# Two-model kernel, one core: top-k rounds spread into the latent attention, the recurrence's mean among its units, a decay parameter and GpSimd's power table at other places, normalisation factors taken one product sooner

## What is computed

```python
score = einsum('bths,bth->bts', relu(iqb @ ik * idx_scale), wb)      # indexer of A, causal
_, sel = lax.top_k(score, topk)                                      # topk = 128
o = o_inter + o_intra ; o = rmsnorm(o, g_out)                        # recurrence B, mean over 64 channels
a_bar = exp(A * dt) ; b_bar = (a_bar - 1) / A * B                    # S5 of the even layer, and powers of a_bar
log_a = -RG_C * gate_r * softplus(-lam) ; a = exp(log_a)             # RG-LRU of the odd layer
```

## Time and profile before

| | us |
|---|---|
| median of 3 runs | 3545.89 (3545.56 to 3547.06) |
| the profiled execution | 3545.3 |
| its span in the profile | 3543.5 |
| PE busy | 3386.2 (96% of the span) |
| DVE, ACT, POOL busy | 1597.8 (45%), 1170.5 (33%), 409.4 (12%) |
| granted TensorE clock, mean | 0.977 of full |

### The profile page before, as it was taken

The page is one execution under the profiler, slowest core; times in us unless marked ns, Lnnn a source line. Parts: engine busy times, 40 slices in busy tenths (PEclk is TensorE's granted clock), DMA queues, the critical chain, the costliest instruction groups (busy, mean ns, idle before and its releaser), DMA issues.

```text
span 3543.5 us, 39704 instructions
## 1 busy us (share of the span) xinstructions
PE 3386.2 (96%) x14384; PEld 2598.6 (73%) x14384; DVE 1597.8 (45%) x2295; ACT 1170.5 (33%) x1727; POOL 409.4 (12%) x285
## 2 busy tenths in 40 slices
PE   7999998999999999999899999899899997899998
PEld 5888775778887888775677887565678885668886
DVE  3332498533323333388734332834333327543322
ACT  4232344433323332244433322213333223543322
POOL 1110002111100110001111100401111002111100
PEclk9999999999999999999999999899999998999999
DMA  4332231033333333232023332430233332123332
GB/s 135 95 95 95 83 79 43 1 89 95 93 92 94 89 95 95 89 84 61 1 66 89 95 95 88 93 74 30 60 89 95 95 94 78 54 75 93 93 95 77
DMA packets 420124, 286.04 MB, mean 81 GB/s; under 512 B 57416, under 2 KB 395180, under 8 KB 419884
## 3 DMA queue, kind: packets, MB, share of 16 engines
q1 hardware_dynamic: 419200, 283.62, 27.8%
q10 hardware_dynamic: 828, 1.13, 0.1%
HBM read 280.24 MB, written 4.47 MB: 80 GB/s over the span
## 4 chain that ended last, share of the span: by engine, by line
PE 89%; DVE 7%; ACT 2%; issue 2%; DMA 0%; POOL 0%; DVEq 0%; ACTq 0%; SPq 0%; POOLq 0%
PE bank L856 25%; PE bank L857 25%; PE bank L858 25%; PE bank L1266 1%; PE bank L1147 1%; PE bank L1165 1%; PE bank L1146 1%; PE bank L851 1%; PE bank L1260 1%; PE bank L1383 1%; DVE small L2078 1%; DVE arena L2080 1%; PE bank L996 0%; PE bank L998 0%; PE bank L997 0%
## 5 line engine op out<-in xcount | busy, mean ns | idle before, releaser
L858 PE MATMUL bank<-xn_lo,w_hi 128*128 128x512 f32 x2800 | 1098.5, 392 | 0.0
L856 PE MATMUL bank<-xn_hi,w_hi 128*128 128x512 f32 x2496 | 1001.5, 401 | 53.6 <-DVE xn_lo L1970 20.3
L1981 DVE TENSOR_TENSOR w_lo<-wring,w_hi 128x1024 fp32r<-128x1024 f32 x478 | 594.6, 1245 | 930.1 <-ACT w_hi L1509 929.2
L857 PE MATMUL bank<-xn_hi,w_lo 128*128 128x512 f32 x2496 | 990.4, 397 | 0.0
L1509 ACT ACTIVATE w_hi<-wring 128x1024 fp32r<-128x1024 f32 x490 | 517.6, 1059 | 1206.2 <-DMA wring<-in_ffn_down 357.9
L858 PEld LDWEIGHTS bank<-xn_lo,w_hi 128*128 128x128 f32 x2800 | 529.5, 189 | 132.8
L856 PEld LDWEIGHTS bank<-xn_hi,w_hi 128*128 128x128 f32 x2496 | 470.5, 188 | 176.8 <-issue 61.3
L857 PEld LDWEIGHTS bank<-xn_hi,w_lo 128*128 128x128 f32 x2496 | 471.4, 189 | 104.7 <-issue 2.6
L857 PE MATMUL bank<-h_hi,w_lo 128*128 (+1 forms) x1056 | 421.3, 399 | 0.0
L856 PE MATMUL bank<-h_hi,w_hi 128*128 (+1 forms) x1056 | 416.1, 394 | 0.0
L858 PE MATMUL bank<-h_lo,w_hi 128*128 (+1 forms) x1056 | 414.0, 392 | 0.0
(11 more groups left out here) (383 smaller groups left out, 2956.2 us busy)
## 6 DMA issues: line engine op xcount, KB each, us to landing
wring<-in_ffn_gate SPq DMA_DIRECT2D x88, 512.0 KB, 3.8
wring<-in_ffn_up SPq DMA_DIRECT2D x88, 512.0 KB, 3.8
wring<-in_ffn_down SPq DMA_DIRECT2D x88, 512.0 KB, 3.5
wring<-in_ffn_w_gate SPq DMA_DIRECT2D x44, 512.0 KB, 3.8
wring<-in_ffn_w_up SPq DMA_DIRECT2D x44, 512.0 KB, 3.8
wring<-in_ffn_w_down SPq DMA_DIRECT2D x44, 512.0 KB, 3.5
wring<-in_w_in SPq DMA_DIRECT2D x34, 512.0 KB, 3.7
wring<-in_w_out SPq DMA_DIRECT2D x16, 512.0 KB, 3.5
```

The source lines that it names most:

```text
L856: nc.tensor.matmul(ps, w_hi[:, slot, t, 0:M], hi, start=start, stop=False)
L857: nc.tensor.matmul(ps, w_lo[:, slot, t, 0:M], hi, start=False, stop=False)
L858: return nc.tensor.matmul(ps, w_hi[:, slot, t, 0:M], lo, start=False, stop=stop)
L1981: nc.vector.tensor_tensor(w_lo[:, slot, :, :].rearrange("p k c -> p (k c)"), wunit[:, slot, :], w_hi[:, slot, :, :].rearrange("p k c -> p ...
```

## The change

Six edits.

1. `Z_RSTD`: ACT takes factors 0 and 1 at unit dcq1, 2 and 3 at dckv, 4 and 5 at bq; none at bk.
2. `act_norm`: the table load for Sigmoid stands before the last chunk's copy, not before the first.
3. Top-k: passes 0 to 8 of the mixers' loop have 2, 2, 1, 1, 1, 1, 1, 1, 1 rounds, then 4 follow, and the last 12 stand one each in the attention's units i = 2 to 13.
4. Recurrence B: its output is made in banks 4 and 5, after one wait for all of DVE's blocks; both means are made in bank 5 at units 3 and 5, the factors on ACT at i = 4 and 6, the norm on DVE at i = 5 and 7. `Y_HYB` puts the convolution's chunks first.
5. The chain on `spc` moves to the even layer: its first two operations ahead of the parameters, the Exp beside them, and the other 17 behind the states, before the rotation of queries and keys.
6. GpSimd's power table waits for DVE's last `x_pow`, not for `par` = 40.

The diff, without the lines that only renumber waits and with the moved chain shortened:

```diff
-Z_RSTD = {"dcq1": (0,), "dckv": (1,), "bq": (2, 3), "bk": (4, 5)}
+Z_RSTD = {"dcq1": (0, 1), "dckv": (2, 3), "bq": (4, 5)}
...
-Y_HYB, Y_EVEN, Y_ODD = [2, 3, 4, 5, 6, 7, 0, 1], [4, 5, 6, 7, 0, 1, 2, 3], list(range(KD))
+Y_HYB, Y_EVEN, Y_ODD = [4, 5, 2, 3, 6, 7, 0, 1], [4, 5, 6, 7, 0, 1, 2, 3], list(range(KD))
...
             pe.e.wait_ge(dh_sq.h, dh_sq.by(pe.l, 16))
+            pe.e.wait_ge(at_sb.h, at_sb.by(pe.l, 2 * TB))
             for pr in range(2):
                 for tb in range(TB):
-                    pe.e.wait_ge(at_sb.h, at_sb.by(pe.l, 2 * (tb + 1)))
...
-                        nc.tensor.matmul(pb[pr][64 * q:64 * q + 64, tb * P:(tb + 1) * P], b_values[:, tb, h * B_VAL:(h + 1) * B_VAL],
+                        nc.tensor.matmul(pb[4 + pr][64 * q:64 * q + 64, tb * P:(tb + 1) * P], b_values[:, tb, h * B_VAL:(h + 1) * B_VAL],
...
-            pe_out_mean(pe, 0)
...
         def pe_out_mean(pe, pr):
 
-            pe.e.wait_ge(o_sq.h, o_sq.by(pe.l, pr + 1))
-            pe.e.wait_ge(u_msk.h, u_msk.by(pe.l, NCH - 1))
-            nc.tensor.matmul(pb[6 + pr][:, :], C("blk64"), T(t_osq[pr]), start=True, stop=True).then_inc(on_ps.h, 1)
+            pe.e.wait_ge(o_sq.h, o_sq.by(pe.l, 2))
+            if pr:
+                pe.e.wait_ge(on_ln.h, on_ln.by(pe.l, 1))
+            nc.tensor.matmul(pb[5][:, :], C("blk64"), T(t_osq[pr]), start=True, stop=True).then_inc(on_ps.h, 1)
...
         def hyb_ready(eng, u):
-            if u == 1:
-                pe_out_mean(eng, 1)
+            if u in (3, 5):
+                pe_out_mean(eng, (u - 3) // 2)
             if u == 2:
+                eng.e.wait_ge(o_sq.h, o_sq.by(eng.l, 1))
...
-            if u == 3:
+            if u == 8:
                 eng.e.wait_ge(on_ln.h, on_ln.by(eng.l, 2))
...
             if st:
-                nc.scalar.preload_act_table(ACT.Sigmoid)
                 for k in range(KD):
+                    if k == KD - 1:
+                        nc.scalar.preload_act_table(ACT.Sigmoid)
...
         def hyb_out_factor(act, i):
-            if i in (1, 2):
-                act.e.wait_ge(on_ps.h, on_ps.by(act.l, i))
-                rstd(act, pb[6 + i - 1][:, :], T(t_or[i - 1]), on_ln, on_r, i)
+            if i in (4, 6):
+                pr = (i - 4) // 2
+                act.e.wait_ge(on_ps.h, on_ps.by(act.l, pr + 1))
+                rstd(act, pb[5][:, :], T(t_or[pr]), on_ln, on_r, pr + 1)
...
             act.e.wait_ge(pro_sb.h, 2 + 4)
             nc.scalar.activation(c_dt, c_ldt, ACT.Exp).then_inc(par_act.h, 1)
+            act.e.wait_ge(sp_step.h, 2)
+            nc.scalar.activation(spc[:, 1, :], spc[:, 0, :], ACT.Exp, scale=-1.0).then_inc(par_act.h, 1)
...
         def act_odd(act):
-            act.e.wait_ge(sp_step.h, 2)
-            nc.scalar.activation(spc[:, 1, :], spc[:, 0, :], ACT.Exp, scale=-1.0).then_inc(par_act.h, 1)
...
         HEAD_TOP = sum(Z_ROUNDS)
-        HEAD_PART = 2
+        HEAD_ROUNDS = [2, 2, 1, 1, 1, 1, 1, 1, 1]
+        HEAD_END = HEAD_TOP + sum(HEAD_ROUNDS)
+        END_ROUNDS = 4
...
-                top = HEAD_TOP + i * HEAD_PART
-                dve_top(dve, top, top + HEAD_PART)
-            dve_top(dve, top + HEAD_PART, 3 * TOP_N)
+                top = HEAD_TOP + sum(HEAD_ROUNDS[:i])
+                dve_top(dve, top, top + HEAD_ROUNDS[i])
+            dve_top(dve, HEAD_END, HEAD_END + END_ROUNDS)
 
         def hyb_out_norm(dve, i):
-            if i in (2, 3):
-                pr = i - 2
+            if i >= 2:
+                top = HEAD_END + END_ROUNDS + i - 2
+                dve_top(dve, top, top + 1)
+            if i in (5, 7):
+                pr = (i - 5) // 2
...
             dve.e.wait_ge(pro_sb.h, 2 + 4)
+            sp_n = count(1)
+            lam = col2[:, R2["rg_lam_2"]:R2["rg_lam_2"] + KD]
+            S = [spc[:, i, :] for i in range(8)]
+            ts(S[2], lam, -1.0, None, ALU.mult).then_inc(sp_step.h, 1)
+            dve.e.wait_ge(sp_step.h, next(sp_n))
+            tt(S[0], lam, S[2], ALU.max).then_inc(sp_step.h, 1)
+            dve.e.wait_ge(sp_step.h, next(sp_n))
...
             state(S5_Q - 1)
             dve.e.wait_ge(q_pow.h, 3 * S5_Q)
+            dve.e.wait_ge(par_act.h, 2)
             ts(S[3], S[1], 2.0, None, ALU.add).then_inc(sp_step.h, 1)
...
-            pool.e.wait_ge(par.h, 40)
+            pool.e.wait_ge(x_pow.h, 3 * S5_Q)
```

More of the change, by code:

```diff
@@ L1662, in act_mixers @@
                 act.e.wait_ge(o_ps.h, o_ps.by(act.l, pr + 1))
-                nc.scalar.activation(T(t_osq[pr]), pb[pr][:, :], ACT.Square)
-                nc.scalar.activation(T(t_o[pr]), pb[pr][:, :], ACT.Copy).then_inc(o_sq.h, 1)
+                nc.scalar.activation(T(t_osq[pr]), pb[4 + pr][:, :], ACT.Square)
+                nc.scalar.activation(T(t_o[pr]), pb[4 + pr][:, :], ACT.Copy).then_inc(o_sq.h, 1)
         def hyb_out_factor(act, i):
-            if i in (1, 2):
-                act.e.wait_ge(on_ps.h, on_ps.by(act.l, i))
-                rstd(act, pb[6 + i - 1][:, :], T(t_or[i - 1]), on_ln, on_r, i)
+            if i in (4, 6):
+                pr = (i - 4) // 2
+                act.e.wait_ge(on_ps.h, on_ps.by(act.l, pr + 1))
+                rstd(act, pb[5][:, :], T(t_or[pr]), on_ln, on_r, pr + 1)
         def act_attention(act, units, ytile, st, order, mixed, then, first=None):
@@ L1719, in hyb_mixed @@
             if n < 2:
-                act.e.wait_ge(y_b.h, y_b.by(act.l, n + 1))
+                act.e.wait_ge(y_conv.h, y_conv.by(act.l, n + 1))
             else:
-                act.e.wait_ge(y_conv.h, y_conv.by(act.l, n - 1))
+                act.e.wait_ge(y_b.h, y_b.by(act.l, n - 1))
         def even_mixed(act, n):
@@ L2348, in dve_even @@
             stt(pow_c, pow_s, 0.25, pow_c, ALU.add, ALU.subtract).then_inc(par.h, 1)
-            dve.e.wait_ge(par_act.h, 6)
+            dve.e.wait_ge(par_act.h, 7)
             tt(c_nre, c_r, c_cos, ALU.mult).then_inc(par.h, 1)
@@ L2386, in dve_even @@
             tt(b2, b2, t2, ALU.subtract).then_inc(par.h, 1)
-            dve.e.wait_ge(par_act.h, 8)
+            dve.e.wait_ge(par_act.h, 9)
             tt(T(e_ar), pow_e, pow_c, ALU.mult).then_inc(par.h, 1)
@@ L2473, in rotated @@
                     dve.e.wait_ge(tab_sin.h, 2)
-                    dve.e.wait_ge(par_act.h, 3)
+                    dve.e.wait_ge(par_act.h, 4)
                 if i == 1:
@@ L2499, in dve_even @@
             dve.e.wait_ge(q_pow.h, 3 * S5_Q)
-            for i in range(8 + 1):
-                if i < 8:
-                    dve.e.wait_ge(rot_ps.h, i + 1)
-                    if i >= 2:
-                        dve.e.wait_ge(rot_ready.h, i - 1)
-                    tt(rope_t[i % 2], pb[2 + 2 * (i % 2)][:, :], T(e_sin), ALU.mult).then_inc(rot_s.h, 1)
-                if i >= 1:
-                    u = i - 1
-                    t = T((e_q if u % 2 == 0 else e_k) + u // 2)
-                    dve.e.wait_ge(rot_s.h, u + 1)
-                    dve.e.wait_ge(rot_c.h, u + 1)
-                    tt(t, t, rope_t[u % 2], ALU.add).then_inc(rot_ready.h, 1)
-        def dve_odd(dve):
-            V = nc.vector
-            ts, tt, stt = V.tensor_scalar, V.tensor_tensor, V.scalar_tensor_tensor
-            dve_units(dve, STAGES["in", "odd"], 2, 4)
-            V.memset(xpad[:, :, 0:LRU_TAPS - 1], 0.0).then_inc(pad_zero.h, 1)
-            sp_n = count(1)
-            lam = col2[:, R2["rg_lam_2"]:R2["rg_lam_2"] + KD]
-            S = [spc[:, i, :] for i in range(8)]
-            ts(S[2], lam, -1.0, None, ALU.mult).then_inc(sp_step.h, 1)
-            dve.e.wait_ge(sp_step.h, next(sp_n))
-            tt(S[0], lam, S[2], ALU.max).then_inc(sp_step.h, 1)
-            dve.e.wait_ge(sp_step.h, next(sp_n))
-            dve.e.wait_ge(par_act.h, 9)
+            dve.e.wait_ge(par_act.h, 2)
             ts(S[3], S[1], 2.0, None, ALU.add).then_inc(sp_step.h, 1)
@@ L2549, in dve_odd @@
             assert next(sp_n) == SP_STEPS + 1
+            for i in range(8 + 1):
+                if i < 8:
+                    dve.e.wait_ge(rot_ps.h, i + 1)
+                    if i >= 2:
+                        dve.e.wait_ge(rot_ready.h, i - 1)
+                    tt(rope_t[i % 2], pb[2 + 2 * (i % 2)][:, :], T(e_sin), ALU.mult).then_inc(rot_s.h, 1)
+                if i >= 1:
+                    u = i - 1
+                    t = T((e_q if u % 2 == 0 else e_k) + u // 2)
+                    dve.e.wait_ge(rot_s.h, u + 1)
+                    dve.e.wait_ge(rot_c.h, u + 1)
+                    tt(t, t, rope_t[u % 2], ALU.add).then_inc(rot_ready.h, 1)
+        def dve_odd(dve):
+            V = nc.vector
+            ts, tt, stt = V.tensor_scalar, V.tensor_tensor, V.scalar_tensor_tensor
+            dve_units(dve, STAGES["in", "odd"], 2, 4)
+            V.memset(xpad[:, :, 0:LRU_TAPS - 1], 0.0).then_inc(pad_zero.h, 1)
             def squares(half):
```

2 lines of the change are left out of this document (1 added, 1 removed).

## The result

The change makes the kernel 1.76% faster: 3483.23 us (median of 4 runs, 3482.08 to 3485.21) against 3545.72 for the kernel before on the same chip (3544.24 to 3547.06), ratio 0.9824, 95% interval 0.9807 to 0.9841. The profiled execution of the changed kernel took 3482.52 (span 3480.7, mean granted clock 0.987; before 3543.5 and 0.977).

The account below looks back on a forecast made before the run. TensorE, busy for 96% of the span, bounds the kernel; each wait costs its length plus lower clock behind it. 1.0 + 11.2 + 8.0 + 14.5 + 13.0 = 47.7 us off 3545.3: 3497.6, median 3498, range 3484 to 3512.

Parts of the forecast that it names:

- The in-projection (edits 1, 2): In-projection, per layer: start 0.5 us sooner, wait before the tok units and its low clock gone, 5.6; twice: 1.0 and 11.2.
- The odd layer (edit 5): Odd layer: L856's wait of 11.4 us and 2.2 of low clock go, weights 0.75 late; 13.0 faster, bounds 9 and 13.8.
- Top-k and the output (edits 3, 4): Mixers and attention: first row maximum 8.3 us sooner, partly given back in the units; 4.0 per layer, 8.0 in all.
- Then L1120's 6.0 (both at the lower clock as now: its wait is still over 5 us): Recurrence's output: L1114 takes 3.8 us, L1120 6.0, both at the lower clock; first scores 0.9 more, at 623.7.
- no longer the bound: Ahead of the first row maximum: DVE finishes its four last rounds at 620, before TensorE's first scores at 623.7.
- About 2.5 come on top at the start: Attention's first units: 2.5 us more, from scores at the lower clock and the first mean (up to 1.8) ahead of unit 3.
- The price of the rounds themselves: Attention's units to 14: 12 rounds of 0.98 add 11.8 us to DVE's 16, making 27.6, so DVE sets the pace.
- GpSimd's table (edit 6): Even layer: DVE's powers run freely, its tables take turns with GpSimd and end at 2295.0; 14.5 us faster, bounds 6 and 25.
- less the lower clock behind the new wait: Even layer: 3.5 us deducted from 18.0 for low clock behind a new wait of 6.5 at "v" 2.
- the other case: Even layer: if TensorE keeps the lower clock in `kt`, it arrives at 2295 itself and nothing changes from 14.5.
- The case of a table that is free: Even layer rival: GpSimd's table fits beside DVE's without turns, "v" 2 does not wait; 10 us more, 3488; chance 0.12.
- The last rival: Attention's units: TensorE, paced by DVE with gaps, stays at the lower clock, up to 22 us a layer; 3550 or more; 0.01.

Follow-up runs that it names:

- the run with four back: Changed kernel with four top-k rounds put back from the attention's units 2 to 5 to ahead of the first row maximum: 3498.3 us, changed kernel 3483.2.
- the run with two more: Changed kernel with two more top-k rounds taken from the mixers' loop, as second rounds at attention units 2 and 3: 3486.9 us, changed kernel beside it 3483.48.

## Why the prediction was right or wrong

**The in-projection (edits 1, 2)** was right: 7.0 and 5.8 for 6.1. The wait goes, the start gives 0.5, the fourth unit's weights are in time. The two layers differ by the low clock in them, 3 and 7 us, and for no other reason that the trace shows.

**The odd layer (edit 5)** was right: 12.7 for 13.0, with GpSimd's split 1.0 late for 0.75.

**Top-k and the output (edits 3, 4)** is the step that failed most, 4.0 a layer for 7.9. Two of its terms were wrong.
- "Then L1120's 6.0 (both at the lower clock as now: its wait is still over 5 us)". The wait is 5.4, as forecast, and L1114's 3.7 as well, but L1120 takes 3.4. That is 2.6 us, of which 2.2 arrive at the first row maximum (52.2 behind L1071, forecast 623.7 - 569.3 = 54.4). It could not have been more, by a second slip: I had DVE's last round end at 620, 50.7 behind L1071, and DVE "no longer the bound". It ends at 52.2, and the row maximum stands directly behind it. Taking L1114 in one piece goes with it: 6.2 falls to 3.95 where one wait takes the place of four and nothing else changes. It is no certainty. Over all profiled runs of this study L1120 takes 3.3 to 4.0 us in 22 of the 24 layers with one wait (6.2 in layer two of the two kernels with second rounds at the first units), and 6.2 in nine of the ten layers with four (3.8 in the tenth). Why, stays open.
- "About 2.5 come on top at the start". They did not. From first row maximum to unit 14's it is 28.1 and not 30.1: the clock is full in the first units, and TensorE waits 0.4 once a layer at the means, where it waits 0.8 and 0.7 when they stand at units 1 and 3. Putting them there made unit 4 3.5 later. That is 2.0 us. The 2.2 and the 2.0 together are what lies between the 7.9 measured and the 3.7 that the sum gave before I rounded it up.

The price of the rounds themselves was not the miss. I had put DVE's work, its idle time filled, at 27.6 us for these units, and they take 28.1. Before it was 25.5, with stalls of its own (ACT's factor, 1.94). That most of a round lies in DVE's idle time agrees with the run with four back, where the units return 0.5 for four rounds, and with the run with two more, where they take 0.9 for two.

**GpSimd's table (edit 6)**: the mechanism was right. DVE and GpSimd take turns wherever both work, so that the sum of their work is kept (4.35 for 2.29 beside operations that take 2.03 alone): the table ends 1.6 us sooner than I put it (2263.88 + 29.75, by which the layer starts sooner, = 2293.6 in the time of before, for 2295.2). What failed is the term behind it, "less the lower clock behind the new wait", 3.5. I had named the other case, TensorE at the lower clock in `kt`, and had written that nothing changes then. It was the case: the clock is 0.57 from 2234 to 2242, TensorE arrives at 2263.6 (2293.4 in the time of before, 4.7 later than forecast), the wait shrinks to 0.26, and so nothing is low behind it. 1.6 + 3.5 = 5.1, for the 5.0 that is missing. In the run with `kt` moved the low clock moved with those tiny products.

The Trainium skill, page "SBUF — State Buffer", section "Who interferes with whom", says that a VectorE instruction with two SBUF inputs, or in a two-port mode, and one of GpSimd that reads SBUF lock each other out for a whole instruction. The runs agree, and show which work pays most for it: eight scans at 12.89 for 1.56 with GpSimd at work, 1.4 us more for each, where a 128x2048 operation, 2.29 us long, pays 2.1. From these two places I would put a table of GpSimd beside few long instructions of VectorE rather than many short ones; no further run tests that.

**The range and the rivals.** The case of a table that is free gave 3488, the right direction for the wrong reason: the table was not free. I had no case in which a shorter wait saves more than its own length and its own low stretch, and each layer's attention was one. The last rival, a clock that stays low through the units, did not come about in the change, but the run with two rounds at units 14 and 15 has one like it: 29 us more in one layer, behind a wait of 1.2. I had thought that DVE would have to hold TensorE up throughout for it; behind that one gap nothing held it up.

The Trainium skill, page "TensorE: Matmul & The Clock Gate", section "What's actually happening", says that the clock follows how busy the engine has lately been, and that the moment of a change depends on where in a free-running interval the work falls. What is seen here is compatible with the second, though no run tests it: the same code behind the same wait is followed by 3 and by 17 us of lower clock in one piece, from one layer to the next, and stretches that no edit touched moved by 2 to 6 us. The first does not explain the run with two rounds at units 14 and 15, where the rows show TensorE busy throughout, for over 60 us, at 0.50.

## What to carry to other kernels

Price a stall of TensorE as its length and what the clock does behind it, counting the low time only where the engine works: here that second part was 27 of 62 us. Look, too, whether the work behind the stall comes in one run or in several pieces. When work is moved into an engine's idle time, ask how much of the saving in front another wait takes back, and what was due at its end: four rounds brought 3.9 us in front, two more only 0.7, and two that made a mask 1.2 us late left the kernel 25 us slower. And judge a part by its own stretch of the timeline, with the granted clock beside it, as a total carries the clock's shifts in stretches that nobody touched.

## What the hardware showed that I had not expected

- Behind a wait of 1.21 us the clock stayed at its lower level for over 60 us, with TensorE busy in all of them; the same wait in the other layer was followed by 14 us of it.
- The same wait before L1114 in both layers had very different low times around it, with the same code: 10 and 17 us up to the attention's end with two further rounds at the first units (wait 5.4), 3 and 31 us with four (wait 3.8).
- In a run of tiny products (64 of 128x16, 0.15 us each) the clock fell with no idle time ahead of it, to 0.57 over the 8 us at their end and behind them, and where they were moved the low clock moved too.
- GpSimd's operations beside eight short scans of VectorE multiplied the scans' time by 8 (12.89 for 1.56) and were themselves hardly slowed (2.0 to 2.5 us each, 2.0 to 2.4 without the scans).
